# Recurrent layer of a two-block transformer: projection units interleaved, one root for two norms, decay arithmetic on ScalarE, three output units accumulated together

## The chip, the core and the metric

The kernel runs on one core of a Trainium2 chip. Times are device microseconds (us) of that core. A core has TensorE (PE, matmuls), VectorE (DVE), ScalarE (ACT), GpSimd (POOL) and SyncE (SP, which here only issues loads). Each engine runs its own list of instructions in order, and engines meet at semaphores: an instruction that waits holds up everything behind it on its engine. Lower is better; the number that counts is the median of repeated executions.

## The reference

Two small networks in a row on 256 tokens (the first one with 16 more in front), model width 1024. The change touches the step from the first to the second: the final norm of the first, and the recurrent block of the second.

```python
# first block ends, second block begins (xt: 256 tokens)
x   = rmsnorm(h, norm_final)                    # the "final" norm
y   = rmsnorm_2(x, a_norm)                      # norm of the recurrent block
u   = y @ w_in                                  # 1024 x 2048
gate, rec = u[..., :1024], u[..., 1024:]
rec = causal_depthwise_conv(rec, conv_w, conv_b)          # 4 taps
g   = einsum('bsnd,nde->bsne', rec_in_8_blocks, w_gate) + b_gate
r, i = sigmoid(g[..., :128]), sigmoid(g[..., 128:])
log_a = -8 * r * softplus(-lam)
a   = exp(log_a)
b   = sqrt(-expm1(2 * log_a)) * (i * rec)
h_t = a_t * h_(t-1) + b_t                       # scan over the tokens
x   = x + (gelu(gate) * h) @ w_out              # 1024 x 1024
x   = x + square(relu(rmsnorm_2(x, mlp_norm) @ w_up)) @ w_down
```

The kernel writes sqrt(1 - a^2) as (1 + a) * sqrt(tanh(-log_a / 2)).

## The kernel before

Activations lie transposed: 128 channels on the partitions, tokens along the row, so a width of 1024 is eight tiles n = 0..7. Every weight matrix is cut into units of 8 tiles of 128x128 (512 KB). Each fp32 product is made of three matmuls of 256 columns (lines 861 to 863): high part of the weight by high and by low part of the activation, and low part of the weight by high part. A unit is thus 24 matmuls, and gives one output tile of 128 channels; `unit` issues it.

Around each unit four engines work in a pipeline over a ring of four slots. SP loads the raw unit (`w_raw`); ACT rounds it to `w_hi` (line 473); DVE subtracts to `w_lo` (line 1319); PE uses both; DVE then reads the PSUM bank `acc` (`scaled`, line 1335, or the residual add, line 1359). The call `ahead(phase, k)` stands in ACT's and DVE's lists where unit k + 3 is split. ACT's split waits until the unit four places back has been used, DVE's for ACT's, and PE's unit for DVE's. The order of everything else on an engine is written out by hand.

The recurrent layer runs in three phases before: `lru_rec` (8 units, the branch that is convolved and scanned, read into `rec`), `lru_mix` (order `LRU_MIX`: two units g0 and g1 with the gate weights, eight units y0 to y7 for the gelu branch, read into `gate2`), and `lru_out` (8 units of the output matrix). After each `rec` tile, ACT makes the first tap of the convolution (line 711), DVE the other three (lines 1733 and 1715) into `xc`, ACT its high part `xc_hi` (704), DVE its low part `xc_lo` (1721). The gate products go through ACT's Sigmoid into `gsig` (725). DVE multiplies by `coef` (`log_decay`, 1742), ACT makes Exp and Tanh (734, 736), DVE clamps (1749), ACT takes the root (742), POOL has made i * xc (443), DVE makes (1 + a) * b (1754), times the root (1761), and the scan (1763). POOL multiplies by gelu (448) into `b_s`; ACT and DVE make `lr_hi` (767) and `lr_lo` (1794), on which `lru_out` waits. A name such as `a_s[:, q, :]` with q of four tiles is one instruction of 1024 columns.

Ahead of that stand the two norms. POOL sums two rows of squares, PE sums them over the partitions (lines 888 and 891). ACT takes a root, DVE its reciprocal (1347), two multiplications (1692, 1693) give the second variance, ACT takes a second root (698), DVE a second reciprocal (1706) and a product (1707). Only then is `rstd`, by which every tile of `rec` is scaled, complete. `normalise` (1699) rewrites `h` tile by tile with the final norm, which the residual adds of `lru_out` need.

## Time and profile before

| quantity | value |
|---|---|
| median of 3 runs | 1265.49 us (1264.58 to 1265.87) |
| the profiled execution's own time | 1259.41 us |
| its span in the trace | 1257.6 us |
| mean granted TensorE clock | 0.988 of full speed |
| PE busy | 1216.7 us (97%) |
| DVE busy | 836.3 us (67%) |
| ACT busy | 679.1 us (54%) |
| POOL busy | 102.3 us (8%) |

The profiled execution took 1.8 us more than its span, and 6.1 us less than the median of the timed runs. Its page says where each engine was busy, and its trace gives every instruction a start and a duration in microseconds from the start of the span. Consecutive instructions of one engine overlap a little, so the distance from one start to the next is what a queue costs. The recurrent layer stands at 657.6 to 755.7 us.

### The profile page before, as it was taken

The numbers are of one execution on the slowest core, as the hardware profiler recorded it, in microseconds if no ns is written. First come the engines' busy times: TensorE is split into PE (matmuls) and PEld (weight loads), VectorE is DVE, ScalarE is ACT, GpSimd is POOL, SyncE is SP. The second block draws the span as 40 slices with busy tenths as digits, with TensorE's granted clock in tenths as the row PEclk, the third lists the DMA queues.
The fourth block names the chain that finished last, engine by engine and source line by source line (L and its number), as shares of the span: only waits on it lengthen the run. The fifth ranks groups of instructions, "written<-read, shape, count | busy, mean of one in ns | idle before, by whom it ended". The sixth has DMA issues, their size and how long they took to land.

```text
span 1257.6 us, 26919 instructions
## 1 busy us (share of the span) xinstructions
PE 1216.7 (97%) x9788; PEld 1175.3 (93%) x9788; DVE 836.3 (67%) x1299; ACT 679.1 (54%) x1095; POOL 102.3 (8%) x116
## 2 busy tenths in 40 slices
PE   8999999999999999999999779999999998999999
PEld 8998999999997799999999779999999967999998
DVE  5677866665578767666669897665565566766543
ACT  5445665644445656665555856554444356655442
POOL 2000200000100210000120230000010022100000
PEclk8999999999999999999999989999999999999999
DMA  6433455556653235555664345556666422655653
GB/s 238 152 117 100 152 183 169 179 170 201 185 205 118 68 117 181 185 185 183 201 201 142 127 146 180 185 187 203 189 223 209 135 68 60 185 183 189 203 187 114
DMA packets 57420, 207.63 MB, mean 165 GB/s; under 512 B 6336, under 2 KB 7552, under 8 KB 57104
## 3 DMA queue, kind: packets, MB, share of 16 engines
q1 hardware_dynamic: 56992, 203.52, 50.7%
q0 software_dynamic: 288, 3.21, 0.6%
q8 instruction: 41, 0.67, 0.2%
q14 instruction: 19, 0.16, 0.0%
q10 hardware_dynamic: 80, 0.07, 0.0%
HBM read 205.66 MB, written 1.05 MB: 164 GB/s over the span
## 4 chain that ended last, share of the span: by engine, by line
PE 87%; DVE 7%; issue 3%; ACT 2%; POOL 1%; DVEq 0%; POOLq 0%; ACTq 0%
PE acc L861 27%; PE acc L863 27%; PE acc L862 26%; DVE w_lo L1319 2%; PE acc L961 1%; PE acc L1144 1%; ACT pe L836 1%; POOL sqsum L406 1%; PE pa L1058 1%; DVE t_s L1763 1%; DVE x_lo L1341 0%; DVE nmx L1895 0%; PE pa L1116 0%; PE pa L1244 0%; PE stat L1217 0%
## 5 line engine op out<-in xcount | busy, mean ns | idle before, releaser
L861 PE MATMUL acc<-x_hi,w_hi 128*128 128x256 f32 (+1 forms) x1784 | 512.2, 287 | 7.9 <-DVE x_lo L1341 4.3
L1319 DVE TENSOR_TENSOR w_lo<-w_raw,w_hi 128x1024 fp32r<-128x1024 f32 x382 | 468.2, 1228 | 74.5 <-ACT w_hi L473 73.7
L863 PE MATMUL acc<-x_hi,w_lo 128*128 128x256 f32 (+1 forms) x1784 | 508.5, 285 | 0.0
L862 PE MATMUL acc<-x_lo,w_hi 128*128 128x256 f32 (+1 forms) x1784 | 508.0, 285 | 0.0
L473 ACT CAST w_hi<-w_raw 128x1024 fp32r<-128x1024 f32 x382 | 397.4, 1045 | 189.9 <-PE acc L863 184.9
L861 PEld LDWEIGHTS acc<-x_hi,w_hi 128*128 128x128 f32 x1784 | 339.2, 190 | 13.4 <-issue 5.6
L863 PEld LDWEIGHTS acc<-x_hi,w_lo 128*128 128x128 f32 x1784 | 339.5, 190 | 0.0
L862 PEld LDWEIGHTS acc<-x_lo,w_hi 128*128 128x128 f32 x1784 | 338.1, 190 | 0.4
L863 PE MATMUL acc<-m_hi,w_lo 128*128 128x256 f32 x512 | 141.4, 276 | 0.0
L861 PE MATMUL acc<-m_hi,w_hi 128*128 128x256 f32 x512 | 141.4, 276 | 0.0
L862 PE MATMUL acc<-m_lo,w_hi 128*128 128x256 f32 x512 | 141.3, 276 | 0.0
L863 PE MATMUL acc<-mid_hi,w_lo 128*128 128x272 f32 (+1 forms) x352 | 100.4, 285 | 0.0
L861 PE MATMUL acc<-mid_hi,w_hi 128*128 128x272 f32 (+1 forms) x352 | 100.3, 285 | 0.0
L862 PE MATMUL acc<-mid_lo,w_hi 128*128 128x272 f32 (+1 forms) x352 | 100.1, 284 | 0.0
L861 PEld LDWEIGHTS acc<-m_hi,w_hi 128*128 128x128 f32 x512 | 96.1, 188 | 0.0
L862 PEld LDWEIGHTS acc<-m_lo,w_hi 128*128 128x128 f32 x512 | 96.1, 188 | 0.0
L863 PEld LDWEIGHTS acc<-m_hi,w_lo 128*128 128x128 f32 x512 | 96.1, 188 | 0.0
L1359 DVE TENSOR_TENSOR h<-h,acc 128x256 f32 (+1 forms) x56 | 23.8, 426 | 90.9 <-PE acc L863 90.4
L490 ACT ACTIVATE sq<-h (+1 forms) x64 | 26.4, 422 | 90.7 <-DVE h L1359 90.7
L861 PEld LDWEIGHTS acc<-mid_hi,w_hi 128*128 128x128 f32 x352 | 66.4, 189 | 0.0
L863 PEld LDWEIGHTS acc<-mid_hi,w_lo 128*128 128x128 f32 x352 | 66.4, 189 | 0.0
L862 PEld LDWEIGHTS acc<-mid_lo,w_hi 128*128 128x128 f32 x352 | 66.3, 188 | 0.0
(302 smaller groups left out, 1570.7 us busy)
## 6 DMA issues: line engine op xcount, KB each, us to landing
w_raw<-weights SPq DMA_DIRECT2D x382, 512.0 KB, 3.5
bias<-bias_rows POOLq DMA_DIRECT2D x1, 2048.0 KB, 8.6
h<-hT SPq DMA_DIRECT2D x4, 272.0 KB, 4.9
bias<-bias_rows POOLq DMA_DIRECT2D x1, 1088.0 KB, 5.9
outT<-h SPq DMA_DIRECT2D x4, 256.0 KB, 4.7
con<-constants SPq DMA_DIRECT2D x1, 913.0 KB, 9.0
par<-cols SPq DMA_DIRECT2D x1, 84.0 KB, 2.0
kidx<-kidx ACTq DMA_DIRECT2D x1, 68.0 KB, 3.3
```

The lines of the kernel that those rows point to most:

```text
L406: pool.tensor_tensor(flat(sqsum[:, tok]), sq[:, bass.ds(n, 1), tok], flat(sqsum[:, tok]), ALU.add)\
L473: nc.scalar.copy(w_hi[:, slot, :], w_raw[:, slot, :]).then_inc(hi_ready, 1)
L490: nc.scalar.activation(sq[:, nn, tok], h[:, nn, tok], ACT.Square).then_inc(sq_ready, 1)
L836: ins = nc.scalar.activation(pe2[:, t % 2, g, 0:n], lg2[:, t % 2, g, 0:n], ACT.Exp, bias=nmx2[:, 2 * t + g:2 * t + g + 1], accum_out=rs2[: ...
L861: nc.tensor.matmul(out, wh, xh[:, k, tok], start=first and n == 0, stop=False)
L862: nc.tensor.matmul(out, wh, xl[:, k, tok], start=False, stop=False)
L863: ins = nc.tensor.matmul(out, wl, xh[:, k, tok], start=False, stop=last and n == ntiles - 1)
L961: ins = nc.tensor.matmul(acc[2 + c % 2][:, m * n:(m + 1) * n], S[:, c % 2, m // 2, (m % 2) * P:(m % 2 + 1) * P], q_T[:, m // 2, lo:hi], st ...
L1058: nc.tensor.matmul(pa[t % 2][:, 0:n], qidx[p0:p0 + IDX_DIM, hd // 2, qt * P:(qt + 1) * P], kidx[p0:p0 + IDX_DIM, 0:n], start=True, stop=Tr ...
L1144: ins = nc.tensor.matmul(acc[hd % 4][:, qt * P:(qt + 1) * P], vh[0:m, b, hd * P:(hd + 1) * P], pt1[0:m, qt, b0:b0 + P], start=(b == 0), st ...
L1319: V.tensor_tensor(w_lo[:, slot, :], w_raw[:, slot, :], w_hi[:, slot, :].bitcast(F32), ALU.subtract)\
L1359: V.tensor_tensor(h[:, nn, tok], h[:, nn, tok], acc[j][:, 0:n_tok].rearrange("p (a t) -> p a t", a=1), ALU.add)\
```

## The change

Five edits.

1. The phases `lru_rec` and `lru_mix` become one phase `lru_in` of 18 units in the order r0 r1 y0 r2 r3 y1 g0 r4 r5 y2 r6 r7 y3 y4 g1 y5 y6 y7. The elementwise work on ACT and DVE is attached to other units of that order.
2. Both norms come from one root: PE adds EPS times the first sum (matrix `tiny`) to the second sum in the same bank, and ACT takes one root with bias EPS squared. The root of the final norm is taken beside it, and its reciprocal and all eight `normalise` move to units g1, y5 and y6.
3. `log_decay` and `clamp` leave DVE. ACT's Exp and Tanh take `coef` and `coef_half` as a scale for each channel, four instructions of 256 columns instead of one of 1024, and the root takes 2^-100 as a bias. Exp, Tanh and root are issued for each half apart.
4. The product with gelu moves from POOL to DVE. (1 + a) * b is made tile by tile just before its scan; the product with the root is made before it.
5. In `lru_out` the first three units run together, k tile by k tile, each k waiting for its `lr_lo`; `lru_out` is written out and not looped.

```diff
+LRU_IN = ["r0", "r1", "y0", "r2", "r3", "y1", "g0", "r4", "r5", "y2", "r6", "r7", "y3", "y4", "g1", "y5", "y6", "y7"]
+OUT_TOGETHER = 3
 ## POOL
-                pool.wait_ge(s_("conv_ready"), KD)
+                pool.wait_ge(s_("conv_ready"), 4 * half + 4)
                 pool.tensor_tensor(b_s[:, q, :], gsig[:, q, SEQ:2 * SEQ], xc[:, q, :], ALU.mult).then_inc(s_("ix"), 1)
-            for n in range(KD):
-                pool.wait_ge(s_("scanned"), n + 1)
-                ...
-                pool.tensor_tensor(b_s[:, n, :], t_s[:, n, :], gelu_s[:, n, :], ALU.mult).then_inc(s_("lru_mid"), 1)
 ## ACT
+            act.wait_ge(s_("sumg_ready"), 1)
+            nc.scalar.activation(std[:, xt], pa[0][:, 0:SEQ], ACT.Sqrt, bias=eps[:, 3:4], scale=1.0 / D)\
+                .then_inc(s_("std_lru"), 1)
+            act.wait_ge(stat_ready, NORM["final"] + 1)
+            nc.scalar.activation(std_final[:, xt], stat[:, 0:SEQ], ACT.Sqrt, bias=eps[:, 0:1], scale=1.0 / D)\
+                .then_inc(std_ready, 1)
+            def half_tanh(half):
+                for n in range(4 * half, 4 * half + 4):
+                    act.wait_ge(s_("gate_read"), n + 1)
+                    nc.scalar.activation(t_s[:, n, :], gsig[:, n, 0:SEQ], ACT.Tanh, scale=coef_half[:, n:n + 1])\
+                        .then_inc(s_("tanh_ready"), 1)
+            def tanh_root(half):
+                act.wait_ge(s_("tanh_ready"), 4 * half + 4)
+                nc.scalar.activation(t_s[:, q, :], t_s[:, q, :], ACT.Sqrt, bias=eps[:, 2:3]).then_inc(s_("tsqrt_ready"), 1)
+            def decay(half):
+                for n in range(4 * half, 4 * half + 4):
+                    nc.scalar.activation(a_s[:, n, :], gsig[:, n, 0:SEQ], ACT.Exp, scale=coef[:, n:n + 1])\
+                        .then_inc(s_("a_ready"), 1)
+            for e, item in enumerate(LRU_IN):
+                if e:
+                    ahead("lru_in", e)
+                if conv is not None:
+                    lead_conv(conv)
+                if kind == "r":
+                    first_tap(n)
+                elif kind == "g":
+                    gates(n)
+                if item == "r4":      half_tanh(0)
+                elif item == "r5":    tanh_root(0)
+                elif item == "y2":    decay(0)
+                elif item == "r6":    gelu(0, 3)
+                elif item == "g1":    half_tanh(1)
+                elif item == "y4":    lead_out(0), lead_out(1), lead_out(2)
+                elif item == "y5":    tanh_root(1)
+                elif item == "y6":    decay(1)
+            gelu(3, 7)
+            gelu(7, 8)
+            ahead("lru_out", 0)
+            for n in range(3, KD):
+                lead_out(n)
 ## PE
+                    nc.tensor.matmul(pa[0][:, 0:SEQ], tiny[:, :], sqsum[:, tok], start=False, stop=True)\
+                        .then_inc(s_("sumg_ready"), 1)
+            for k in range(KD):
+                pe.wait_ge(s_("lr_ready"), k + 1)
+                for m in range(OUT_TOGETHER):
+                    if k == 0:
+                        pe.wait_ge(lo_ready, u + m + 1)
+                        pe.wait_ge(acc_free, MT["lru_out"] + m - 3)
+                    ...  (three matmuls into acc[m])
+            for m in range(OUT_TOGETHER, KD):
+                pe.wait_ge(acc_free, MT["lru_out"] + m - 3)
+                unit(u + m, (u + m) % RING, acc[m % 4][:, 0:SEQ], lr_hi, lr_lo, st, True, True)
 ## DVE
+            def drive(half):
+                dve.wait_ge(s_("ix"), half + 1)
+                dve.wait_ge(s_("tsqrt_ready"), half + 1)
+                V.tensor_tensor(b_s[:, q, :], b_s[:, q, :], t_s[:, q, :], ALU.mult).then_inc(s_("driven"), 1)
+            def recur(n):
+                dve.wait_ge(s_("driven"), n // 4 + 1)
+                dve.wait_ge(s_("a_ready"), n + 1)
+                own_wait(dve, V.scalar_tensor_tensor(out=b_s[:, n, :], in0=a_s[:, n, :], scalar=1.0, in1=b_s[:, n, :],
+                                                     op0=ALU.add, op1=ALU.mult))
+                V.tensor_tensor_scan(t_s[:, n, :], a_s[:, n, :], b_s[:, n, :], 0.0, ALU.mult, ALU.add)\
+                    .then_inc(s_("scanned"), 1)
+            def gate_recurrence(n): ...   # b_s = t_s * gelu_s, lru_mid
+            def trail_out(n): ...         # lr_lo = b_s - lr_hi, lr_ready
+            for e, item in enumerate(LRU_IN):
+                if kind != "g":
+                    unit_done("lru_in", e)
+                    scaled(out, acc[b % 4][:, 0:SEQ], xt)
+                if conv is not None:
+                    trail_conv(conv)
+                if e:
+                    ahead("lru_in", e)
+                if kind == "r":
+                    taps(n)
+                if item == "y2":      drive(0)
+                elif item == "r6":    recur(0), recur(1)
+                elif item == "y3":    recur(2), recur(3)
+                elif item == "y4":    gate_recurrence(0), (1), (2)
+                elif item == "g1":    trail_out(0), (1), (2), invert_final()
+                elif item == "y5":    normalise(0) ... normalise(3)
+                elif item == "y6":    normalise(4) ... normalise(7), drive(1)
+            ahead("lru_out", 0)
+            recur(4)
+            gate_recurrence(3)
+            recur(5)
+            gate_recurrence(4)
+            trail_out(3)
+            ...
+            gate_recurrence(7)
+            trail_out(6)
+            trail_out(7)
```

(The branches of the two loops are put on one line each here.)

Where instructions stand on ACT, from the second Sigmoid group on. `gsig` are the two sigmoids, `t_s` the tanh and its root, `a_s` the decay, `gate` the gelu. Before:

```order
L473 CAST w_hi<-w_raw 128x1024 x2
L734 ACT_TABLE_LOAD
L734 ACTIVATE a_s<-t_s 128x1024
L736 ACTIVATE t_s<-t_s 128x1024
L734 ACTIVATE a_s<-t_s 128x1024
L736 ACTIVATE t_s<-t_s 128x1024
L473 CAST w_hi<-w_raw 128x1024
L742 ACT_TABLE_LOAD
L742 ACTIVATE t_s<-t_s 128x1024 x2
L473 CAST w_hi<-w_raw 128x1024
L746 ACT_TABLE_LOAD
```

And now, from the first three high parts of the product with gelu on:

```order
L748 CAST lr_hi<-b_s 128x256 x3
L472 CAST w_hi<-w_raw 128x1024
L718 ACT_TABLE_LOAD
L718 ACTIVATE gsig<-pa,par 128x256 x4
L718 ACTIVATE gsig<-pt,par 128x256 x2
L718 ACTIVATE gsig<-stat,par 128x256 x2
L727 ACTIVATE t_s<-gsig,coef_half 128x256 x4
L472 CAST w_hi<-w_raw 128x1024
L734 ACT_TABLE_LOAD
L734 ACTIVATE t_s<-t_s,eps 128x1024
L472 CAST w_hi<-w_raw 128x1024
L738 ACT_TABLE_LOAD
L738 ACTIVATE a_s<-gsig,coef 128x256 x4
```
Behind these rows follow one more `w_hi`, the load for Gelu and the two gelus. Before, both halves share one table load for each function; now each half has its own, with a `w_hi` between one function and the next. In the whole layer the loads go from 5 to 9.

On DVE, from the last read of the gelu branch to the last `lr_lo`. Before:

```order
L1335 TENSOR_TENSOR gate<-acc,rstd 128x256
L1319 TENSOR_TENSOR w_lo<-w_raw,w_hi 128x1024
L1794 TENSOR_TENSOR lr_lo<-b_s,lr_hi 128x256 x8
L1319 TENSOR_TENSOR w_lo<-w_raw,w_hi 128x1024 x2
L1699 SCALAR_TENSOR_TENSOR h<-h,par,rstd_final 128x256 x5
```

And now (`SCALAR_TENSOR_TENSOR t_s<-a_s,b_s` is the scan):

```order
L1378 TENSOR_TENSOR gate<-acc,rstd 128x256
L1362 TENSOR_TENSOR w_lo<-w_raw,w_hi 128x1024 x2
L1776 SCALAR_TENSOR_TENSOR b_s<-a_s,b_s 128x256
L1778 SCALAR_TENSOR_TENSOR t_s<-a_s,b_s 128x256
L1784 TENSOR_TENSOR b_s<-t_s,gate 128x256
L1776 SCALAR_TENSOR_TENSOR b_s<-a_s,b_s 128x256
L1778 SCALAR_TENSOR_TENSOR t_s<-a_s,b_s 128x256
L1784 TENSOR_TENSOR b_s<-t_s,gate 128x256
L1788 TENSOR_TENSOR lr_lo<-b_s,lr_hi 128x256
```
Before, all eight scans stood ahead of the last read; now the scans of tiles 4 to 7 stand behind it, and behind two `w_lo`, the second of which (`ahead("lru_out", 0)`) waits for ACT's `w_hi` behind the second gelu.

On PE, where the output units begin (buffer numbers shown). Before, one unit runs through its eight k tiles:

```order
L863 MATMUL acc3<-x_hi,w_lo 128x256
L896 UNCONDITIONAL_BRANCH
L896 ISA
L854 REGISTER_ALU
L861 MATMUL acc0<-lr_hi,w_hi 128x256
L862 MATMUL acc0<-lr_lo,w_hi 128x256
L863 MATMUL acc0<-lr_hi,w_lo 128x256
L861 MATMUL acc0<-lr_hi,w_hi 128x256
```

And now, three units share each k tile:

```order
L883 MATMUL acc3<-x_hi,w_lo 128x256
L1228 MATMUL acc0<-lr_hi,w_hi 128x256
L1229 MATMUL acc0<-lr_lo,w_hi 128x256
L1230 MATMUL acc0<-lr_hi,w_lo 128x256
L1228 MATMUL acc1<-lr_hi,w_hi 128x256
L1229 MATMUL acc1<-lr_lo,w_hi 128x256
L1230 MATMUL acc1<-lr_hi,w_lo 128x256
L1228 MATMUL acc2<-lr_hi,w_hi 128x256
L1229 MATMUL acc2<-lr_lo,w_hi 128x256
L1230 MATMUL acc2<-lr_hi,w_lo 128x256
L1228 MATMUL acc0<-lr_hi,w_hi 128x256
```
The third and later groups of a k tile need the `w_lo` of the second and third output unit, which before were needed 24 and 48 matmuls later.

## Rows read from the trace of the kernel before

**Rows 1.** The profile's page, part 1: span and DVE's busy time.
```profile
span 1257.6 us, 26919 instructions
PE 1216.7 (97%) x9788; PEld 1175.3 (93%) x9788; DVE 836.3 (67%) x1299; ACT 679.1 (54%) x1095; POOL 102.3 (8%) x116
```
**Rows 2.** Table of windows, two stretches: us; PE, PEld, DVE, ACT, POOL busy (instructions); clock, DMA.
```profile
657.59:755.72 98.13, 80.56 (x632) 78.67 (x631) 87.62 (x135) 63.03 (x99) 20.87 (x18) 0.93 0.44 139
664.47:728.97 64.50, 48.94 (x389) 47.50 (x387) 57.39 (x93) 41.41 (x61) 13.43 (x10) 0.94 0.37 118
```
**Rows 3.** Timeline, PE: start, duration, instruction, in brackets idle time and releaser.
```profile
730.81 0.55 PE L861 MATMUL acc<-lr_hi,w_hi 128*128 128x256 f32 x1 [10.48 <-DVE lr_lo L1794]
...
735.00 0.41 PE L862 MATMUL acc<-lr_lo,w_hi 128*128 128x256 f32 x1
735.21 0.37 PE L863 MATMUL acc<-lr_hi,w_lo 128*128 128x256 f32 x1
...
755.44 0.28 PE L863 MATMUL acc<-lr_hi,w_lo 128*128 128x256 f32 x1
...
758.38 0.39 PE L861 MATMUL acc<-x_hi,w_hi 128*128 128x256 f32 x1 [0.17 <-DVE x_lo L1341]
```
**Rows 4.** Timeline, DVE, the norms and the first convolutions.
```profile
662.68 1.75 DVE L1347 RECIPROCAL rstd<-std 128x256 f32<-128x256 f32 x1 [0.65 <-ACT std L494]
...
670.40 0.42 DVE L1335 TENSOR_TENSOR rec<-acc,rstd 128x256 f32<-128x256 f32 x1
671.56 0.48 DVE L1733 SCALAR_TENSOR_TENSOR cv<-rec,par,cv 128x256 f32<-128x256 f32 x1 [0.74 <-ACT cv L711]
672.08 0.48 DVE L1715 SCALAR_TENSOR_TENSOR cv<-rec,par,cv 128x256 f32<-128x256 f32 x1
672.49 0.42 DVE L1335 TENSOR_TENSOR rec<-acc,rstd 128x256 f32<-128x256 f32 x1
672.82 0.48 DVE L1715 SCALAR_TENSOR_TENSOR xc<-rec,par,cv 128x256 f32<-128x256 f32 x1
673.21 1.22 DVE L1319 TENSOR_TENSOR w_lo<-w_raw,w_hi 128x1024 fp32r<-128x1024 f32 x1
674.35 0.48 DVE L1733 SCALAR_TENSOR_TENSOR cv<-rec,par,cv 128x256 f32<-128x256 f32 x1
```
**Rows 5.** Chain of waits, the first scans: start, us, engine, what, line.
```profile
718.51 0.04 DVE t_s L1763
...
719.12 2.81 DVE t_s L1763 x3
```
**Rows 6.** Timeline, DVE, beside POOL's products and after.
```profile
699.08 2.56 DVE L1319 TENSOR_TENSOR w_lo<-w_raw,w_hi 128x1024 fp32r<-128x1024 f32 x1 [3.94 <-ACT w_hi L473]
...
730.24 2.77 DVE L1794 TENSOR_TENSOR lr_lo<-b_s,lr_hi 128x256 fp32r<-128x256 f32 x8
```
**Rows 7.** Timeline, POOL: one product i * xc, and products with gelu.
```profile
698.18 2.37 POOL L443 TENSOR_TENSOR b_s<-gsig,xc 128x1024 f32<-128x1024 f32 x1 [37.23 <-ACT gsig L725]
...
719.28 4.82 POOL L448 TENSOR_TENSOR b_s<-t_s,gate 128x256 f32<-128x256 f32 x4 [13.90 <-DVE t_s L1763]
```
**Rows 8.** Timeline, ACT, the second half of the layer.
```profile
695.08 1.57 ACT L725 ACTIVATE gsig<-pa,par 128x256 f32<-128x256 f32 x4
...
697.95 2.04 ACT L473 CAST w_hi<-w_raw 128x1024 fp32r<-128x1024 f32 x2
...
714.72 1.03 ACT L473 CAST w_hi<-w_raw 128x1024 fp32r<-128x1024 f32 x1
715.77 1.28 ACT L746 ACT_TABLE_LOAD   x1
717.06 1.06 ACT L746 ACTIVATE gate<-gate 128x1024 f32<-128x1024 f32 x1
...
728.97 2.54 ACT L767 CAST lr_hi<-b_s 128x256 fp32r<-128x256 f32 x8
...
738.50 0.50 ACT L486 ACTIVATE x_hi<-h,par  x1
```

More of the change, by code:

```diff
@@ L155, in build @@
         sqg_sum = rstd_final
[L156 removed]
+        std_final = sq[:, 1, :]
         par = sb("par", [P, NCOLS])
@@ L704, in lead_conv @@
                 nc.scalar.copy(xc_hi[:, n, :], xc[:, n, :]).then_inc(s_("xc_hi_ready"), 1)
-            for n in range(KD):
-                if 1 <= n <= KD - 2:
-                    ahead("lru_rec", n + 1)
-                act.wait_ge(acc_free, tile_read("lru_rec", n))
-                nc.scalar.activation(cv[:, n % 2, 0, :], rec[:, n, 0:SEQ], ACT.Identity, scale=col("conv_w", n),
-                                     bias=col("conv_b", n)).then_inc(s_("tap0_ready"), 1)
-                if n:
-                    lead_conv(n - 1)
-            ahead("lru_mix", 0)
-            lead_conv(KD - 1)
             def gates(half):
@@ L772, in relu_mlp @@
+            gelu(3, 7)
[3 more added lines that the diff above has]
+                lead_out(n)
+            for n in range(KD):
+                if n < KD - 1:
+                    ahead("lru_out", n + 1)
+                act.wait_ge(acc_free, tile_read("lru_out", n))
+                square(n, xt)
+                make_x("mlp_norm0", n, xt)
             def relu_mlp(layer, norm):
@@ new lines, in _ @@
+            ahead("lru_out", 0)
[4 more added lines that the diff above has]
+            trail_out(3)
+            recur(6)
+            gate_recurrence(5)
+            trail_out(4)
+            recur(7)
+            gate_recurrence(6)
+            trail_out(5)
+            gate_recurrence(7)
+            trail_out(6)
+            trail_out(7)
+            dve.wait_ge(s_("final_h"), KD)
+            for n in range(KD):
+                unit_done("lru_out", n)
+                V.tensor_tensor(h[:, n, xt], h[:, n, xt], acc[n % 4][:, 0:SEQ], ALU.add).then_inc(acc_free, 1)
+                if n < KD - 1:
+                    ahead("lru_out", n + 1)
+                make_x_lo("mlp_norm0", n, xt, XN["mlp0"])
```

269 lines of the change are left out of this document (120 added, 149 removed).

## The prediction

> **What bounds the kernel now.** I read the page first: PE is busy for 1216.7 of 1257.6 us [rows 1], so only the places where it stands still matter, and of those only the ones that this change touches. The table of windows gives the recurrent layer 98.13 us from its first matmul to the end of its last [rows 2]. It has 26 units of 24 matmuls. Twenty-odd matmuls after the idle time PE runs at one in 0.118 us: from the start at 735.21 to the one at 755.44 are 171 steps [rows 3], so a unit costs 2.84 us and 26 units 74 us. Some 24 us of the layer are thus waits or slow clock. The largest is 10.48 us ahead of the first output unit, and the releaser is DVE's `lr_lo` [rows 3].
>
> The second view is DVE's column over 664.47 to 728.97, the time from the first reciprocal to ACT's first `lr_hi`: 57.39 of 64.50 us busy [rows 2]. PE has 48.94 there. So the layer is not bound by PE but by the DVE queue, and mixing units cannot bring more than the queue's idle time and its lost work. I therefore work out the new DVE queue, with ACT's beside it, and look at PE only where one of them waits for it.
>
> **Prices, start to start.** A PSUM read 0.33, a tap 0.40, but 0.52 where it waits for the one just before; `w_lo` 1.14 [rows 4]. `xc_lo`, `lr_lo` and the product with gelu are of the kind and size of the read: 0.34. A scan 0.61 [rows 5]; with (1 + a) * b ahead of it, which it waits for (0.52), a tile costs 1.13. The product with the root has the size of `w_lo`: 1.2. On ACT: `w_hi` 1.0 (two in 2.04), eight sigmoids 2.87 (695.08 to 697.95), a table load 1.28, 1024 columns about 1.0, 256 columns with a scale for each channel 0.40 (the 0.50 us `x_hi` less the overlap), `lr_hi` 0.31 [rows 8].
>
> **The norms.** Before, the first `rec` read is at 670.40; the first reciprocal starts at 662.68 and takes 1.75 [rows 4]. Now this one reciprocal gives `rstd`, so DVE starts at 664.5, 5.9 us earlier. The extra `tiny` matmul stands on PE where the second sum stood and costs at most 0.5 us of PE, which has slack. The second reciprocal is not saved: it moves to g1.
>
> **DVE, first part.** A step with a `rec` unit is: read 0.34, `xc_lo` of the tile before with a wait of about 0.2 for ACT 0.55, `w_lo` 1.14, taps 0.52 + 0.52 + 0.40; together 3.45. A gelu unit costs 2.0 behind a `rec` unit and 1.5 otherwise. r0 2.5 (0.75 waiting for ACT's tap, as the 0.74 in rows 4), r1 3.45, y0 2.0, r2 2.9, r3 3.45, y1 2.0, g0's `w_lo` 1.1: DVE is at 682.0. PE has reached g0 at 677 and waits for `xc_lo` of tile 3, so r4 ends at 683.9. That is PE's 1.6 us and DVE's 1.8.
>
> **Second part.** ACT makes its sigmoids until 684.7, then the `w_hi` that r4's `w_lo` needs (685.7). At 684.8 POOL starts its 2.37 us product [rows 7]. In the trace of before a `w_lo` issued 0.9 us into this product took 2.56 us instead of 1.22 and ended 1.1 us after it [rows 6, 7]: DVE stood until POOL was done. So `w_lo` starts at 687.2. Then r4 to its end 2.6 (689.8), r5 3.45, y2 with 0.9 of waiting for ACT's `xc_hi`, the product with the root (697.1), r6 with a wait of 0.8 (700.8), two scans 2.3, r7 3.2, y3 2.0, two scans 2.3 (710.6), y4 1.5, three products 1.0: 713.1, and the first of them is done at 712.5. The queue is full from 687 on.
>
> The Trainium skill, "SBUF — State Buffer" (SBUF: two separate sides), says that VectorE with two SBUF inputs and GpSimd share one pair of ports as an exclusive lock held for the whole instruction. The row of 2.56 us agrees. If they shared bandwidth instead, this term would be about 1.4 us smaller.
>
> **Third part, ACT's string.** ACT's three `lr_hi` wait for that first product. Behind them stand, with no slack: 3 `lr_hi` 0.9, `w_hi` 1.0, load 1.28, sigmoids 2.87, four tanh 1.6, `w_hi` 1.0, load 1.28, root 1.0, `w_hi` 1.0, load 1.28, four Exp 1.6, `w_hi` 1.0, load 1.28, gelu of four and of one tile 1.3, `w_hi` 1.04. Sum 19.5, so 712.6 + 19.5 = 732.1. Four of the layer's nine loads stand here; before it had five in all. DVE's work meanwhile (six `w_lo`, `lr_lo`, the second reciprocal, eight `normalise`, the product with the root, three reads) fits: it waits about 6 us in four pieces, the last for the `w_hi` behind the gelus, which holds up the scans of tiles 4 to 7. POOL's second product falls into such a wait.
>
> **Fourth part.** DVE from 732.1: `w_lo` 1.14, four tiles 4.5, five products with gelu 1.7, five `lr_lo` 1.7 and a wait of 0.2, the last one done at 741.5. PE may do k tile 5 from 740.4 on and then needs 9 matmuls for each k, 1.07 us: k 5, 6 and 7 end at 743.6. Five units at 2.84 give 757.8, and the last matmul's own length 758.0. Before, this moment is 755.44 + 0.28 = 755.7 [rows 3]. What follows (last add, `x_hi`, `x_lo`, PE again at 758.38, 2.7 us after) has the same length. Balance: +2.3 us. `lru_out` itself gets shorter, 8 units in 22.7 us from one `lr_lo` become 5 units and 3.2 us; what eats it is that the last `lr_lo` is 8.5 us later than before (730.24 + 2.77 = 733.0 [rows 6]).
>
> **Not priced.** The memsets at the start lie under the first loads, `coef_half` is 8 columns; nothing for both, 0.1 us if not. SP's loads: a raw slot is free when its `w_lo` is done, at least 6 us ahead of the `w_hi` in my queue.
>
> **Bounds.** Not shown before: tanh and Exp of 256 columns with a scale. Taken 0.40 (`x_hi`); by an unscaled copy 0.31 the string is 0.7 shorter; by the sigmoids with bias from PSUM 0.36; upwards 0.51, as if it also had a bias, 0.9 longer. Scans 0.61, since POOL no longer runs beside; beside POOL's products four scans took 2.81 for three, 0.94 each: +1.3 for the last four. POOL's block in the second part: 0 to 2.4, taken 1.4, the nearest row. PE's clock: after its 10.48 us of idle time 21 matmuls stood 0.21 apart instead of 0.118 [rows 3], 2.0 us in all. Now PE has broken work from 719 to 741; the slow stretch may be over in time, taken 0, or cost up to 2.0. POOL's block alone moves the sum by -1.4 or +1.0. Together the bounds are 0 and +7.5 around a sum of +2.3.
>
> **Rivals.** (a) Slower, clearly: PE's clock is down when the three joint units end, and all 21 slow matmuls fall on the last five units. Place 743 us, price 2.0, total +4.3; it decides if PE's work between 722 and 741, in pieces of three and nine matmuls, doesn't count as work. For it: 21 slow matmuls after the one long wait. Against it: from k 3 on PE is busy for 1.07 of each 1.8 us.
>
> (b) Slower: a change of tables empties the engine as well, so that each load costs more than its 1.28 us. Priced with the length of the longest instruction that would have to drain, the 1.06 us of a gelu [rows 8], the four loads of the string give 4.2, total +6.5. Against it: the load starts 0.02 behind the `w_hi` before it, and the gelu 0.01 behind the load [rows 8]. It decides only if the new order waits where the old one did not; chance small.
>
> The Trainium skill, "ScalarE: Activation LUTs" (What ACT_TABLE_LOAD costs), states 1283 ns for the load and a drain of 1380 ns for every switch; by that page the string would be 5.5 us longer and the total +7.8, an estimate. The trace agrees with the load and shows no drain.
>
> (c) Faster: the string doesn't hold DVE, because ACT's loads or sigmoids start earlier than I let them (they wait for the product of y4 only through three `lr_hi`). Without DVE's 6 us of waiting in the third part the end is 6 us earlier: -3.7. For it: nothing but these small copies ties the two. Against it: they stand ahead of the sigmoids in ACT's list.
>
> (d) Much faster: PE is never held up, the layer takes its 74 us and some 4 of norms and tail, -20. Against it: DVE's own work from 664.5 to the last `lr_lo` adds up to 63 us (77 less the 14 of waits above), so even with no wait at all the last `lr_lo` comes at 727.5 and the end is 14 earlier: -12. That bounds this case.
>
> (e) The order of the joint units gives nothing, since their start waits for the second and third `w_lo` (the third at 730.2): it costs nothing either, because `lr_lo` of tile 3 comes at 736.6.
>
> **How the numbers follow.** The trace's execution took 1259.41 us; +2.3 makes 1261.7. The median shown is 6.1 higher, 1265.49, so the forecast is 1267.8. A measurement of this kernel can tell about 0.2% from no change, 2.5 us: my sum lies just inside. Chances: the sum as worked out 0.60 (its own range 1266 to 1270; 0.34 within 0.2%, 0.25 above, 0.01 below), (a) 0.16 (1269.8; 0.14 slower), (b) 0.03 (1272.0), (c) 0.13 (1261.8; 0.10 faster, 0.03 same), (d) 0.04 (1253.5 at best), something unseen 0.04. Faster 0.15, same 0.43, slower 0.42. The range takes in the bounds and most of (a) and (c): 1261.8 to 1271.5.
>
> **What would show it.** First `rec` read at about 664.5. DVE without idle time from 687 to 713, one `w_lo` of about 2.6 us at POOL's product. ACT without a gap from 712.6 to 732, with four loads. DVE waiting for `w_hi` just ahead of the scans of tiles 4 to 7. Last `lr_lo` near 741.5, PE's three joint units ending near 743.6. The forecast is wrong if the last `lr_lo` ends before 738 or if ACT has idle time in that string; it is too low if matmuls stand 0.21 apart after 743.6.

## The result, and the profile after

The changed kernel takes 1281.19 us (median of 4 runs, 1273.99 to 1283.03) against 1265.03 for the kernel before in the same comparison: a ratio of 1.0131, 95% interval 1.0104 to 1.0157. It is slower by 16 us. The forecast was 1267.8 us, +2.3, with a range up to 1271.5, so the measured time lies 9.7 us above the range. In some executions of these kernels (four of the first ten of b_norm, its profiled one too) PE's clock stays low in the sparse attention, far ahead of the layer, which adds 10 to 20 us; the ratios leave out those over 1.5% above the fastest.

Its profiled execution took 1282.97 us. The page of the changed kernel, span, engines, and PE's granted clock in 40 slices:

```profile
span 1281.2 us, 26855 instructions
PE 1240.5 (97%) x9790; PEld 1196.7 (93%) x9790; DVE 832.6 (65%) x1303; ACT 688.1 (54%) x1111; POOL 94.0 (7%) x108
PEclk8999999999999999999999789999999988999999
```

PE is busy for 23.8 us more than in [rows 1], with two more matmuls. So matmuls run slower; waits are not the main thing. Where the time is shows when the stages are laid side by side. A stage's length here runs from its first matmul to the first one of the next stage (of the last stage, to the end of its last matmul). The column a_1024 is the profile of an experiment told below: the same kernel with 480 bytes of unused memory in front of its later tensors.

| stage (length in us) | before | after | a_1024 |
|---|---|---|---|
| all ahead of the recurrent layer | 657.59 | 661.50 | 657.40 |
| recurrent layer | 97.97 | 101.36 | 101.34 |
| first MLP, input units | 91.71 | 93.22 | 93.22 |
| first MLP, output units | 87.06 | 90.88 | 87.06 |
| kv2 | 50.03 | 50.02 | 50.04 |
| q2, second attention, o2 | 91.12 | 98.28 | 94.14 |
| second MLP, input units | 91.75 | 91.71 | 91.72 |
| second MLP, output units | 87.23 | 91.04 | 87.22 |

The code ahead of the layer is the same in all three; its 3.9 us are an accident of one execution: the first stage takes 106 to 109 us in different executions, and b_scan3, which is the kernel before up to its end, also reaches the layer at 661.5. The layer itself is 3.4 us longer and the stage behind it 1.5: 4.9 us that belong to the change as the prediction looked at it. One profile is one execution: the unchanged layer took 97.8 to 98.4 us in eight profiles, the changed one 101.4, 101.3, 100.3 and 99.8 in four (after, a_1024, a_576, a_late), so its 3.4 us is the upper end of 1.4 to 3.6. The rest, 3.8 us in each of two output stages and 7.2 in the second attention, lies in code that the diff does not touch. The table of windows over the first MLP's output units, of before and then of after (us; PE, PEld, DVE, ACT, POOL busy with instructions; clock; DMA share and rate):

```profile
847.27:934.50 87.23, 87.23 (x772) 87.23 (x771) 47.90 (x49) 39.48 (x48) 5.58 (x6) 1.00 0.64 198
```

```profile
856.08:947.12 91.04, 91.04 (x772) 91.04 (x771) 47.88 (x49) 39.43 (x48) 5.59 (x6) 1.00 0.60 190
```

The same 772 instructions, clock 1.00 in both, PE never idle, and 3.8 us more (these two include the last matmul's own length, the table's row for this stage doesn't). One matmul to the next is 0.1134 us before and 0.118 after.

The layer after, by the same view (it answers to the first line of [rows 2]), and four pieces of the timeline. DVE, from the norm to the last `lr_lo` and the residual steps behind:

```profile
661.50:763.02 101.52, 84.92 (x634) 82.40 (x633) 82.55 (x135) 70.79 (x113) 11.83 (x9) 0.88 0.41 134
```

```profile
666.65 1.75 DVE L1737 RECIPROCAL rstd<-std 128x256 f32<-128x256 f32 x1 [0.68 <-ACT std L696]
668.44 0.43 DVE L1378 TENSOR_TENSOR rec<-acc,rstd 128x256 f32<-128x256 f32 x1
...
687.83 0.42 DVE L1378 TENSOR_TENSOR rec<-acc,rstd 128x256 f32<-128x256 f32 x1 [1.64 <-PE acc L883]
689.73 2.60 DVE L1362 TENSOR_TENSOR w_lo<-w_raw,w_hi 128x1024 fp32r<-128x1024 f32 x1 [1.48 <-ACT w_hi L472]
...
715.93 1.09 DVE L1784 TENSOR_TENSOR b_s<-t_s,gate 128x256 f32<-128x256 f32 x3
...
736.27 1.22 DVE L1362 TENSOR_TENSOR w_lo<-w_raw,w_hi 128x1024 fp32r<-128x1024 f32 x1 [2.16 <-ACT w_hi L472]
...
744.26 0.98 DVE L1788 TENSOR_TENSOR lr_lo<-b_s,lr_hi 128x256 fp32r<-128x256 f32 x2
748.29 0.42 DVE L1847 TENSOR_TENSOR h<-h,acc 128x256 f32<-128x256 f32 x1 [3.05 <-PE acc L1230]
...
765.00 0.41 DVE L1847 TENSOR_TENSOR h<-h,acc 128x256 f32<-128x256 f32 x1
766.30 0.83 DVE L1384 SCALAR_TENSOR_TENSOR x_lo<-h,par,x_hi 128x256 fp32r<-128x256 f32 x1 [0.88 <-ACT x_hi L485]
```

ACT's string, its beginning and its last instruction, and POOL's first product:

```profile
710.78 1.04 ACT L472 CAST w_hi<-w_raw 128x1024 fp32r<-128x1024 f32 x1
716.39 1.08 ACT L748 CAST lr_hi<-b_s 128x256 fp32r<-128x256 f32 x3 [4.56 <-DVE b_s L1784]
717.37 1.04 ACT L472 CAST w_hi<-w_raw 128x1024 fp32r<-128x1024 f32 x1
718.43 1.28 ACT L718 ACT_TABLE_LOAD   x1
...
722.60 1.74 ACT L727 ACTIVATE t_s<-gsig,coef_half 128x256 f32<-128x256 f32 x4
724.19 1.08 ACT L472 CAST w_hi<-w_raw 128x1024 fp32r<-128x1024 f32 x1
725.29 1.28 ACT L734 ACT_TABLE_LOAD   x1
726.59 1.15 ACT L734 ACTIVATE t_s<-t_s,eps 128x1024 f32<-128x1024 f32 x1
...
735.21 1.03 ACT L472 CAST w_hi<-w_raw 128x1024 fp32r<-128x1024 f32 x1
```

```profile
688.84 2.40 POOL L446 TENSOR_TENSOR b_s<-gsig,xc 128x1024 f32<-128x1024 f32 x1 [23.98 <-ACT gsig L718]
```

PE, the joint units and the end of the layer, which answers to [rows 3]:

```profile
734.17 0.58 PE L1228 MATMUL acc<-lr_hi,w_hi 128*128 128x256 f32 x1 [3.18 <-DVE w_lo L1362]
...
740.64 0.58 PE L1228 MATMUL acc<-lr_hi,w_hi 128*128 128x256 f32 x1 [1.62 <-DVE lr_lo L1788]
741.02 0.41 PE L1229 MATMUL acc<-lr_lo,w_hi 128*128 128x256 f32 x1
741.23 0.41 PE L1230 MATMUL acc<-lr_hi,w_lo 128*128 128x256 f32 x1
...
762.74 0.28 PE L883 MATMUL acc<-lr_hi,w_lo 128*128 128x256 f32 x1
...
767.18 0.39 PE L881 MATMUL acc<-x_hi,w_hi 128*128 128x256 f32 x1 [1.43 <-DVE x_lo L1384]
```

### The profile page after: what moved, and what is told of

It reads as the page before. It is cut to its first block, busy times and chain, and to the rows that moved or that the text cites. A ratio compares the mean times of both kernels' runs of the same rounds, so it can differ in the third digit from the quotient of the medians.

```text
span 1281.2 us, 26855 instructions
## 1 busy us (share of the span) xinstructions
PE 1240.5 (97%) x9790; PEld 1196.7 (93%) x9790; DVE 832.6 (65%) x1303; ACT 688.1 (54%) x1111; POOL 94.0 (7%) x108
## 4 chain that ended last, share of the span: by engine, by line
PE 86%; DVE 7%; ACT 3%; issue 3%; POOL 1%; DVEq 0%; POOLq 0%; ACTq 0%
PE acc L881 26%; PE acc L883 26%; PE acc L882 26%; DVE w_lo L1362 2%; DVE x_lo L1384 1%; ACT w_hi L472 1%; PE acc L984 1%; PE acc L1167 1%; POOL sqsum L409 1%; PE pa L1081 1%; DVE cv L1747 1%; PE acc L928 0%; ACT gsig L718 0%; PE pa L1139 0%; PE pa L1287 0%
## 5 line engine op out<-in xcount | busy, mean ns | idle before, releaser
L1402 DVE TENSOR_TENSOR h<-h,acc 128x256 f32 (+1 forms) x48 | 20.5, 427 | 94.4 <-PE acc L883 94.4
L489 ACT ACTIVATE sq<-h (+2 forms) x64 | 26.5, 423 | 90.2 <-DVE h L1402 85.4
```

The costliest lines, as they stand in the source:

```text
L489: nc.scalar.activation(sq[:, nn, tok], h[:, nn, tok], ACT.Square).then_inc(sq_ready, 1)
L1402: V.tensor_tensor(h[:, nn, tok], h[:, nn, tok], acc[j][:, 0:n_tok].rearrange("p (a t) -> p a t", a=1), ALU.add)\
```

## The experiments

**1. The memory alone (b_544).** The kernel before, with two unused tensors where the changed kernel has its new ones. Every tensor declared behind them moves by 544 bytes. (The change also widens `eps` from 2 to 4 columns; b_norm, which has that and 1024 bytes, keeps its output stages at 87.2 us, so it adds nothing to the displacement.)

```diff
+        tiny = sb("tiny", [P, P])
+        coef_half = sb("coef_half", [P, KD])
```

> The kernel before with two unused tensors of 512 and 32 bytes a partition in the places where the changed kernel allocates tiny and coef_half, so that every tensor allocated behind them lies 544 bytes further on, and not one instruction differs. Theory 1 (placement): in the changed kernel the 1536 matmuls on m_hi/m_lo stand 0.118 us apart instead of 0.113, and those on xq_hi/xq_lo 0.119 instead of 0.115, because of this shift. Then they do so here too, each m stretch takes about 90.9 us instead of 87.2, and the kernel is 8 to 9 us slower than before. Theory 2 (the pace follows from what the recurrent layer did earlier, or is chance): m stretches 87.2 us, time within 1 us of before.

Measured: 1270.06 us against 1263.32, ratio 1.0049 (1.0031 to 1.0068), 6.7 us where 8 to 9 were expected. The output stages take 91.04 us each, last matmul included, against 87.23. Not one instruction of the layer differs, and the two stages are as slow as in the changed kernel. Shown: the placement costs these 7.6 us. The matmuls of `q2` and `o2` (on `xq_hi`, `xq_lo`) stand 0.118 us apart instead of 0.114, as expected; that makes q2 0.4 us longer, and the whole second attention takes 92.5 us at full clock against 91.1 (up to 92.1 in other profiles at full clock).

**2. The changed kernel at other addresses (a_576, a_1024).** One more unused tensor behind `coef_half`, of 32 and of 480 bytes.

```diff
         coef_half = sb("coef_half", [P, KD])
+        shift = sb("shift", [P, 8])      # a_576;  [P, 120] in a_1024
```

> The changed kernel with 32 more unused bytes behind coef_half: the tensors behind lie 576 bytes (nine times 64) further on than before instead of 544, so that m_hi begins again at a multiple of 64 bytes. If the pace depends on the place within 64 bytes, the m stretches are back at 87.2 us and the kernel is 8 us faster than the changed one; if it depends on a larger block or on something else, they stay at 90.9.

> The changed kernel with 480 more unused bytes: all tensors behind lie 1024 bytes further on than before. Placement by any power of two up to 1024 gives the m stretches back, 87.2 us each, and xq as before: 8 us faster than the changed kernel, so about 1273. What remains against before is then the recurrent layer (+3.4 us, +1.5 us at the first unit behind it) and the slow clock near the second attention (+7 us), if that stays. Theory 2: no change against the changed kernel.

Measured: a_576 1280.77 us, ratio 1.0123 (1.0081 to 1.0166); its output stages, 92.31 us, are slower still. a_1024 1268.26, ratio 1.0046 (1.0032 to 1.0060), 4.7 us less than the 1273 expected; output stages 87.23 us. So 64 bytes of alignment are no cure, 1024 are. The medians of after and a_1024 are 12.9 us apart, and only part of that is shown to be placement. Their two profiles are 15.9 apart: 7.6 in these stages, 4.1 in the second attention (taken up in 8), and 4.1 ahead of the layer, where the code is the same. What is left of the change is +4.9 us by the medians, 5.8 by the ratio; the table has 3.4 and 1.5 in the layer and behind it.

**3. The joint units (a_tog1).**

```diff
-OUT_TOGETHER = 3
+OUT_TOGETHER = 1
```

> The changed kernel with OUT_TOGETHER = 1: the first output unit alone runs as the low parts come, the other seven after it. By my queue the joint units save two units of 2.84 us less the 2.1 us by which the last three k steps are longer: the layer becomes 4 to 5 us longer than the changed one's. If PE's broken work at a third of its pace was what kept its clock low behind the joint units, it could be as little as 2.

Measured: 1284.04 us, ratio 1.0167 (1.0137 to 1.0197). The layer takes 106.06 us, 4.7 more than with three joint units; the next stage is back at 91.66. The joint units are worth what was expected of them; they lose 1.6 of it behind.

**4. The copies that tie ACT to DVE (a_lead).** a_1024, with ACT's three small `lr_hi` copies moved, and DVE's three `lr_lo` one unit later.

```diff
 # ACT: from y4, ahead of g1's sigmoids, to behind g1's tanh
-                elif item == "y4":
                     for k in range(3):
                         lead_out(k)
 # DVE: from g1 to y5, ahead of normalise
                 elif item == "g1":
+                    invert_final()
+                elif item == "y5":
                     for k in range(3):
                         trail_out(k)
-                    invert_final()
-                elif item == "y5":
```

> The changed kernel with its operands moved by 480 bytes more (a_1024), and the three lr_hi copies that ACT makes ahead of g1's sigmoids put behind g1's tanh; DVE's three lr_lo follow one unit later. Theory: it is these copies that tie ACT's string of 20 us to DVE's queue (ACT stands idle for 4.56 us ahead of them in the changed kernel). Then the string starts at about 714 instead of 716.4 on the changed kernel's clock, is 0.9 shorter, and the last lr_lo comes about 4.9 us earlier: 1263.5 against a_1024's 1268.3, with a_1024's 4.9 us of loss gone. Rival: the string is tied to PE and DVE otherwise too (g1's matmuls, POOL's product, DVE waiting for w_hi), so that the last lr_lo moves by less than 1 us and the time stays at 1268.

Measured: 1262.63 us, ratio 1.0003 (0.9990 to 1.0017), which is 5.6 under a_1024. ACT in a_lead, the tanh, the three copies behind it and the end of the string:

```profile
712.65 1.75 ACT L728 ACTIVATE t_s<-gsig,coef_half 128x256 f32<-128x256 f32 x4
714.25 1.05 ACT L749 CAST lr_hi<-b_s 128x256 fp32r<-128x256 f32 x3
715.16 1.09 ACT L473 CAST w_hi<-w_raw 128x1024 fp32r<-128x1024 f32 x1
...
726.19 1.03 ACT L473 CAST w_hi<-w_raw 128x1024 fp32r<-128x1024 f32 x1
```

The idle 4.56 us are gone. Counted from the layer's first matmul (657.21 here, 661.50 after), the string ends at 70.0 us instead of 74.7, the last `lr_lo` at 79.0 instead of 83.7, and the layer takes 95.25 us instead of 101.34. The queue gives 4.7 of these 6.1 us. The other 1.4 are PE's clock: in the changed kernel the last part of the joint units ran at its lower level, here at full speed. Two windows of the joint units' last part, of after and then of a_lead:

```profile
744.00:746.50 2.50, 2.50 (x13) 2.50 (x13) 1.11 (x4) 0.52 (x2) 0.00 (x0) 0.50 0.00 0
```

```profile
731.60:738.30 6.70, 5.90 (x45) 5.50 (x46) 4.83 (x12) 1.71 (x5) 0.00 (x0) 1.00 0.01 3
```

Shown: three copies of 0.3 us in the wrong place of ACT's list turn a layer that is 2.7 us shorter than before into one that is 3.4 longer, the clock's share included.

**5. The pile behind the joint units (a_lead2).** a_lead with `OUT_TOGETHER = 2`.

> a_lead with two joint units instead of three. Theory (DVE's eight residual steps of 2.35 us pile up behind the three units that end together, and reach the first stage of the MLP as a wait of 1.4 us for the last x_lo): that wait falls to about 0.2, the MLP's first stage takes 91.9 us instead of 93.4, the layer gets 1 to 2 us longer, and the time stays within 1 us of a_lead's 1262.6. Rival (the wait comes from ACT's x_hi or from POOL's sums and not from the pile): it stays at 1.4 us, and the time grows by the 1 to 2 us of the layer.

Measured: 1262.45 us, ratio 1.0000 (0.9987 to 1.0014). PE's waits in a_lead, 650 to 770 us (what, for whom; total, times, longest), then in a_lead2:

```profile
PE acc L881 <- DVE x_lo L1384: 1.6, 2, 1.4
```

```profile
PE acc L881 <- DVE x_lo L1384: 0.2, 1, 0.2
```

The next stage takes 91.63 us, against 93.21. A residual step costs DVE 2.39 us (748.29 to 765.00 in the changed kernel are seven), PE's unit 2.84: eight steps that begin when three units end at once last there until 4 us after PE's last matmul. Shown: the wait goes with the third joint unit. The layer got 3.6 us longer, not 1 to 2: the two joint units' matmuls of the last k tiles stand 0.21 us apart, at a clock of 0.50, where a_lead's three had 1.00. That the total didn't grow has two causes in these profiles: 1.6 us come back in the next stage, and 2.7 in the second attention, 92.1 us here and 94.8 in a_lead's.

**6. One part alone (b_norm, b_norm_r).** The kernel before with edit 2 only, later tensors moved by 1024 bytes; the final reciprocal and five `normalise` in DVE's idle 3.94 us of [rows 6].

```diff
-            inverse("final", xt)
-            ...  (two products for the second variance, second root, second reciprocal, product)
+            dve.wait_ge(s_("std_lru"), 1)
+            own_wait(dve, V.reciprocal(rstd[:, xt], std[:, xt]))
 ...
+                if item == "y0":
+                    invert_final()
+                    for n in range(5):
+                        normalise(n)
```

> The kernel before with one part of the change alone: both norms from one root (tiny matmul), the final reciprocal and five normalise in DVE's idle 3.94 us at the first gelu unit, and 1024 bytes of displacement for the later tensors, so that placement stays as good. Theory: in the kernel before the first rec read waits for two roots and two reciprocals, and DVE's queue bounds the layer from there, so the layer gets shorter by nearly the 5.9 us that the first reciprocal comes earlier: 1258 to 1260 against 1263.3 to 1265. Rival: ACT's string of sigmoids, Exp, Tanh and roots or PE bounds the layer after the rec units, and no more than 1 or 2 us are gained: 1262 to 1264.

> b_norm once more, since its profiled execution held 17 us of slow PE clock in the sparse attention, far ahead of the layer. Theory: its layer takes 93.0 us as before, against 98.0, and its executions without that slow stretch lie 4 to 5 us under the kernel before. Rival: what the layer gains is given back in the second attention, whose length moves with the moment at which it starts (92 to 95 us), and the median is only 1 to 3 us under the kernel before.

Measured: 1262.78 us, ratio 1.0016 (0.9984 to 1.0047), and the second time 1261.64, ratio 0.9982 (0.9952 to 1.0012). The layer takes 92.99 and 93.97 us in the two profiles against 97.97: 4 to 5 us are won there. In the total no gain is clear of noise, since both intervals contain 1; the medians suggest 0 to 2 us. One place that takes back is the second attention of b_norm_r, 95.4 us long against 91.1. The theory holds for the layer, the rival is nearer for the total.

**7. A better tail (b_tail).** b_norm, gate tiles read ahead of the scans, `lr_lo` of tiles 0 to 3 ahead of the scans of 4 to 7, two joint units, written out as in the change. ACT's list changes with it: two `w_hi` and the first four `lr_hi` move ahead of the last gelu. DVE's new order:

```diff
-                elif item == "y5":
-                    recur(0)
-                elif item == "y6":
-                    recur(1)
-            ahead("lru_mix", LAST_OWN)
-            ...  (eight lr_lo, then two ahead)
+                elif item == "y5":
+                    rooted(0)
+                elif item == "y6":
+                    for n in range(4):
+                        scan(n)
+            ahead("lru_mix", LAST_OWN)
+            ahead("lru_mix", LAST_OWN + 1)
+            rooted(1)
+            for n in range(4):
+                trail_out(n)
+            for n in range(4, 7):
+                scan(n)
+            trail_out(4)
+            scan(7)
+            trail_out(5)
+            ahead("lru_mix", LAST_OWN + 2)
+            trail_out(6)
+            trail_out(7)
```

> b_norm (one root for both norms, later tensors moved by 1024 bytes) with a new tail of the layer: gate tiles are read before the scans, the lr_lo of tiles 0 to 3 stand ahead of the scans of 4 to 7, and two output units run together, k tile by k tile. Theory (DVE's queue bounds the tail too, and its eight residual steps of 2.35 us each must not pile up behind the joint units): the joint units end about 1.4 us after where lru_out's first unit ended its wait plus 4, six units follow, and the next stage starts 4 to 5 us earlier than in b_norm: layer 88 to 89 us instead of 93.0, time 4 us under b_norm, 1256 to 1259. Rival: the joint units meet a slow PE clock or DVE's pile as in the changed kernel, and the layer stays at 92 to 93: no better than b_norm.

Measured: 1255.48 us, ratio 0.9939 (0.9917 to 0.9960). It beats both kernels: by the ratio 8 us under the one before, by the medians 26 under the changed one. PE in b_tail at the joint units and at the end:

```profile
724.57 0.58 PE L1213 MATMUL acc<-lr_hi,w_hi 128*128 128x256 f32 x1 [6.57 <-DVE lr_lo L1793]
...
732.12 0.39 PE L1213 MATMUL acc<-lr_hi,w_hi 128*128 128x256 f32 x1 [0.46 <-DVE lr_lo L1793]
...
753.26 0.39 PE L870 MATMUL acc<-x_hi,w_hi 128*128 128x256 f32 x1 [0.18 <-DVE x_lo L1369]
```

The wait ahead of `lru_out`, 10.48 us in [rows 3], is 6.57. The layer takes 91.21 us, not 88 to 89: 1.8 to 2.8 less than b_norm where 4 to 5 were expected.

**8. The second attention (b_late, a_late).** PE gets small matmuls on the ones matrix ahead of kv2, so that the second attention starts later.

```diff
             relu_mlp(0, "mlp0")
+            keep_warm(pt, 68)      # b_late, kernel before;  43 in a_late, on a_1024
```

> The kernel before with 68 small matmuls (136 issues) of the ones matrix on PE ahead of the second kv2 stage, some 12.5 us of PE work, so that the second attention starts where it does in the changed kernel, at about 997 us. Theory (phase): the chip lowers PE's clock in the second attention according to when it comes, and then this kernel shows the stretches of 0.50 to 0.67 in the q2 and attention stretch too, which takes 97 to 98 us instead of 91.1: 1265.5 + 12.5 + 6 = 1284. Rival (placement or load of this stretch): the clock stays at 1.00 there as in the kernel before and the stretch takes 91 us: 1278.

> a_1024 with 43 small matmuls of the ones matrix ahead of kv2, 8 us of PE work: the second attention starts at 997 instead of 989 us with operands where a_1024 has them. Theory (phase): the stretch from xq takes 97 to 98 us instead of 94.1, and the time is 1268.3 + 8 + 3.5 = 1280. Rival (placement): it stays at 94 or less, 1276.

Measured: b_late 1277.84 us, 14.8 over the kernel before, where the added matmuls take 15.1 us and not 12.5; a_late 1279.05, 10.8 over a_1024 for 9.5 us of added matmuls. The stretch from q2 to o2 takes 94.2 us (start at 999.9) against 91.1, and 97.8 (start at 999.3) against 94.1. a_late comes out as its theory says; b_late's time is its rival's, and its stretch lies between the two. Windows of PE's low clock in the changed kernel, and the second of them in the kernel before:

```profile
1033.00:1045.00 12.00, 11.69 (x57) 8.65 (x58) 7.00 (x21) 4.38 (x18) 2.26 (x3) 0.57 0.09 38
1065.00:1077.00 12.00, 9.37 (x64) 7.94 (x63) 2.74 (x6) 4.74 (x13) 1.04 (x1) 0.72 0.01 1
```

```profile
1065.00:1077.00 12.00, 12.00 (x107) 12.00 (x107) 10.87 (x14) 7.66 (x14) 3.61 (x4) 1.00 0.63 196
```

Both delayed kernels got 3 to 4 us longer there in their profiles, which speaks for the moment. But the same program took 92.0 us (b_norm, start 998.0) and 95.4 (b_norm_r, start 982.0), and the four profiles at 97 to 98 us are all of the changed code. The length of this stretch runs from 91.1 to 98.3 us over the eighteen profiles, and it goes with the clock granted in it:

| the second attention | us | mean granted clock |
|---|---|---|
| before | 91.1 | 1.00 |
| b_norm | 92.0 | 1.00 |
| b_544 | 92.5 | 1.00 |
| a_1024 | 94.1 | 0.95 |
| b_late | 94.2 | 0.95 |
| b_norm_r | 95.4 | 0.95 |
| a_late | 97.8 | 0.91 |
| after | 98.3 | 0.91 |

So placement explains at most 1.4 us here (b_544), and a_late has the changed kernel's length and clock with its operands in good places. What lowers the clock in one execution and not in another stays open.

**9. Which addresses (b_1024, b_256, b_scan, b_scan2, b_scan3).** The kernel before with an unused tensor of 1024 or 256 bytes; and with groups of 48 matmuls behind its end, on PE alone, that read `m_hi` and `m_lo` at a displacement.

```diff
+                        o = k * SEQ + d // 4
+                        nc.tensor.matmul(pt[:, 0:SEQ], wh, mh[:, o:o + SEQ], start=True, stop=True)
+                        ...  (the same with m_lo and with the low weights)
```

> The kernel before with nothing but an unused tensor of 1024 bytes in front of the later tensors. Theory (only the address modulo 1024 counts): the output stages of both MLPs take 87.2 us, and the time is that of the kernel before, within 0.2%. Rival (any displacement costs): 91 us each and +5 to 8 us in the end.

> The kernel before, and behind its last stage 32 groups of 48 matmuls on PE alone that read m_hi and m_lo at addresses moved by 0, 32, 64, ... 992 bytes, with the weights of ring slots 0 and 1; no other engine works then. Theory (the address of the moving operand modulo 1024 sets the pace of these matmuls by itself): start to start 0.113 to 0.114 us at 0, 0.118 at 544, 0.120 at 576, other values at the rest. Rival (the pace of the MLP's output stage comes from what ACT and DVE write at the same time): all 32 groups run at one pace.

> As b_scan, with 20 groups of 48 matmuls on PE alone. The displacement of the high and of the low operand by group: 0, 256, 0, 1024, 4, 8, 16, 0, (32 high only), (32 low only), 0 with ring slots 2 and 3, 32 with slots 2 and 3, 2048, 512, 0, 1056, (0 and 1024), (0 and 256), (256 and 0), 0. Theory (the address modulo 1024): 0.1134 us in each group with 0, also after others, with 1024, 2048 and (0, 1024), and 0.118 to 0.120 with 256, 512 and 1056. Rival (a pace kept from the stage before, lost at the first other address): 0.1134 in the first group alone, and about 0.118 in every later one, those with 0 and 1024 too.

> As b_scan2, 22 groups of 48 matmuls on PE alone, displacement of both operands by group: 0, 224, 256, 256, 0, 16, 256, 32, 256, 224, 0, 96, 1024, 0, then 0 and 0 with ring slots 2 and 3, 0 with slots 0 and 1, 256 with slots 2 and 3, 256, 480, 512, 0 with slots 0 and 1. Theory (history): a group at a multiple of 256 runs at 0.113 where it follows 0, 16, 32 or 1056, and stays at 0.118 where it follows 224 or 480. Rival (the address modulo 256 alone, and b_scan was disturbed): all groups at a multiple of 256 with slots 0 and 1 run at 0.113, also behind 224 and 480.

> The kernel before with an unused tensor of 256 bytes in front of the later tensors. Theory (modulo 256, as most of b_scan2 says): the output stages of both MLPs take 87.2 us each as before. Rival (modulo 1024, as b_scan says): 90.5 to 91 us each.

Measured: b_1024 1263.76 us, ratio 1.0002 (0.9987 to 1.0017). Its output stages take 87.23 us, and those of b_256 (a single execution, 1264.90 us) too, as the theory of a block of 256 bytes says. The first matmuls of four groups of b_scan2: displacement 0, 1024, 4, and 8 bytes.

```profile
1289.08 0.28 PE L1323 MATMUL pt<-m_hi,w_hi 128*128 128x256 f32 x1
...
1294.52 0.28 PE L1323 MATMUL pt<-m_hi,w_hi 128*128 128x256 f32 x1
...
1299.96 0.28 PE L1323 MATMUL pt<-m_hi,w_hi 128*128 128x256 f32 x1
...
1305.80 0.28 PE L1323 MATMUL pt<-m_hi,w_hi 128*128 128x256 f32 x1
```

48 matmuls take 5.44 us at 0 and at 1024 bytes, 5.84 at 4 bytes. By start to start:

| displacement of both operands, bytes | us a matmul |
|---|---|
| 0, 256, 512, 1024, 2048 (b_scan2, b_scan3: 28 groups of 29, slots 0 to 3) | 0.113 to 0.114 |
| 0 with ring slots 2 and 3, once, behind groups at 32 | 0.118 |
| 4; 8; 16 | 0.122; 0.120; 0.119 |
| 32, 1056 | 0.118 |
| 96, 224, 480 | 0.117 |
| b_scan: 0, then 31 steps of 32 up to 992 | 0.113, then 0.118 to 0.120, with 256, 512 and 768 at 0.118 |

No other engine works there, and the clock is full: the address alone slows these matmuls, by 3 to 7%. The 31 displaced groups of b_scan repeat every 256 bytes within 0.0001 us, and its 0.1183 at 544 and 0.1199 at 576 bytes, times 768, are the 91 and 92 us of the output stages. Both operands count (32 bytes on one alone give 0.118 or 0.119). No address off the multiples of 256 ever gave 0.113. At the multiples both paces exist: b_scan ran them at 0.118, b_scan3 at 0.113 also straight behind 224 and 480, so the group just before doesn't decide it, as one theory had it. b_scan2 refutes both of its theories: the block of 1024 bytes, since 256 and 512 give 0.113, and the pace that is lost at the first other address, since it comes back. What decides between the two paces stays open. Nor is 0.113 the pace of every stage at its old address: the matmuls on `lr_hi` and `lr_lo` stand 0.1178 us apart in the kernel before, in b_1024 and in b_544 alike, and 0.120 in a_576.

## Why the prediction was wrong, step by step

To compare times in the layer, 3.9 us are taken off those of the profile after, the difference of the layer's starts.

- **Norms.** First `rec` read at 664.5, forecast 664.5. Right.
- **First and second part.** `w_lo` beside POOL's product: 2.60 us, done 1.1 us after POOL. The forecast let it start its 1.14 us when POOL was done, at 687.2; it ends at 688.4, so that is right. The waits ahead of it, 1.64 and 1.48 us, are near the 1.8 and 1.5 of the working, and the three products end at 713.1, as forecast. The Trainium skill, "SBUF — State Buffer" (SBUF: two separate sides), calls the port an exclusive lock; the trace agrees (2.60 us beside 2.40).
- **ACT's string.** From 712.5 to 732.3, forecast 712.6 to 732.1; four loads, no gap. Right. a_lead shows that the copies (c) named were the real tie: without them the last `lr_lo` comes 4.7 us earlier and the layer is 6.1 us shorter. (c) itself didn't happen in the changed kernel, nor did (d).
- **Rival (b).** The load at 725.29 begins 0.02 us behind the `w_hi`, the root 0.02 behind the load. The drain of 1380 ns that the Trainium skill, "ScalarE: Activation LUTs" (What ACT_TABLE_LOAD costs), states for every switch is not in this trace; it agrees with the load.
- **Fourth part.** Last `lr_lo` done at 741.3, forecast 741.5. The joint units end at 744.8, not 743.6: rival (a) in small. Their last matmuls stand 0.21 us apart from 740.64 on in the profile of after, as in the rows above, with a granted clock of 0.50, but the slow stretch ends before the five last units. "Taken 0" was thus 1.2 us in this execution and explains the +3.4 of the layer beside the +2.3 of the sum. In a_late, where the layer's code is the same, the clock is back 3 us earlier and the layer takes 99.8 us: there 0 was right.
- **Rival (e).** PE starts on the third unit at 730.3, forecast 730.2. But "gives nothing" is wrong: a_tog1 loses 4.7 us of the layer without the joint units, which the sum itself had counted.
- **The tail.** "What follows has the same length": wrong by 1.5 us. This is the step where the 2.4 us of DVE for each residual step was not held against three units that end together; a_lead2 shows it.
- **"Not priced."** This is the step that failed. It counted what the new tensors hold (`coef_half` "is 8 columns; nothing") and the memsets that fill them, and not that 544 bytes in front move every later tensor. A term put at nothing cost 7.6 us in the two output stages, three times the whole sum, and between 0.4 and 1.4 in the second attention. b_544 has it without any of the change: 6.7 us in its time.
- **The range.** It was said to take in the bounds; +7.5 on 1265.5 is 1273.0, and it ended at 1271.5. That decides nothing here.

How far this accounts for the 16 us: about 8 to 9 are placement, 4.9 the layer and the stage behind it. The rest, 2 to 3 us, isn't shown to belong to the change; the low clock in the second attention, which is long in all three profiles of the changed kernel at displaced addresses and in a_late, is the likely place.

With the placement restored the forecast would have held: a_1024, at 1268.26, is within its range and 4.9 us over its kernel before, where the sum said +2.3. That rival (a)'s +4.3 is nearer is luck: its 2.0 us on the last five units didn't come, 1.2 in the joint units and 1.5 behind the layer did.

## What to carry to other kernels

An added tensor is part of a change even if it is tiny: compare the addresses of what PE reads before and after, and pad so that they move by a multiple of 256 bytes (b_256 and b_1024 keep the old pace), then time the change itself. In a list of in-order engines a copy of 0.3 us that waits costs what stands behind it, so look at each small waiting instruction that a new order puts ahead of a long string. Units that end together hand their followers all their work at once: let as many end together as the following engine can take in before the producer is done. Here that is two; with three the total was the same.

## What the runs showed of the hardware

The pace of the MLP's fp32r matmuls of 256 columns at full clock depends on where the moving operand lies: 0.1134 us at its old address and, but for b_scan, at multiples of 256 bytes from it, 0.117 to 0.122 elsewhere, with PE alone at work. For an output stage of 768 matmuls that is 87.2 us against 91.0 at 544 bytes and 92.3 at 576. And the granted clock in the second attention differs between executions and kernels, from a mean of 1.00 to 0.91, and with it the length of a stage that nobody changed, by up to 7 us.
